# A two-layer encoder trunk: opening by halves of the features, another order of bands, halved weight splits and more banks

## The reference

```
cond = silu(c)
mod = cond @ ada_w[l] + ada_b[l]            # 6 groups of 1024: sh1 sc1 g1 sh2 sc2 g2
h = rms_norm(x, g) * (1 + sc1) + sh1
y = layer 0: stick-breaking heads (8) and sliding-window heads (8), one projection in, one out
    layer 1: HGRN2 gated linear recurrence (8 heads of 128), projections in and out
x = x + g1 * y
h = rms_norm(x, g) * (1 + sc2) + sh2
x = x + g2 * ((gelu(conv3(h @ W_gate)) * (h @ W_up)) @ W_down)      # width 2816
```

## Time and profile before

| | us |
|---|---|
| median of 3 runs | 1402.93 |
| their range | 1402.37 to 1403.20 |
| profiled execution | 1405.01 |
| its span | 1403.2 |
| TensorE busy | 1330.3 (95%) |
| VectorE busy | 810.3 (58%) |
| ScalarE busy | 554.9 (40%) |

### The profile page before, as it was taken

One profiled execution on the slowest core, in us unless ns is written; L12 is line 12 of the kernel. 1 busy time (PEld: TensorE's weight loads), 2 busy tenths in 40 slices (PEclk: granted clock), 3 DMA queues, 4 the chain that ended last, 5 costly groups with the idle time before them and its releaser, 6 DMA issues.

```text
span 1403.2 us, 17286 instructions
## 1 busy us (share of the span) xinstructions
PE 1330.3 (95%) x6208; PEld 1085.9 (77%) x6208; DVE 810.3 (58%) x1190; ACT 554.9 (40%) x831; POOL 49.7 (4%) x95
## 2 busy tenths in 40 slices
PE   4899996898999999999989999998999999999997
PEld 3677775676888888887868888887778888888785
DVE  6565356656666655535677777775665555452323
ACT  5455464324333333212155555553243333332213
POOL 1000000000000000000100000000000000000000
PEclk7799998999999999999989999999999999999999
DMA  9333431042545454464822222223523333333232
GB/s 362 109 114 87 127 119 50 1 137 88 161 138 146 141 154 142 136 192 138 269 62 76 75 75 65 72 61 96 174 75 90 99 95 94 100 91 104 79 101 75
DMA packets 189267, 160.37 MB, mean 114 GB/s; under 512 B 4959, under 2 KB 164920, under 8 KB 189218
## 3 DMA queue, kind: packets, MB, share of 16 engines
q1 hardware_dynamic: 177008, 116.41, 27.5%
q0 software_dynamic: 11936, 43.14, 9.9%
q10 hardware_dynamic: 274, 0.16, 0.0%
HBM read 157.59 MB, written 2.10 MB: 114 GB/s over the span
## 4 chain that ended last, share of the span: by engine, by line
PE 88%; DVE 4%; ACT 3%; DMA 1%; issue 1%; SPq 1%; DVEq 0%; ACTq 0%
PE proj L1372 59%; PE z L1372 22%; PE obank L1372 3%; PE misc L1372 2%; DMA w_raw<-ab_w_in 1%; SPq L439 1%; ACT w_hi L559 1%; DVE soft L1033 0%; DVE w_lo L881 0%; ACT q_sb L646 0%; ACT soft_a L646 0%; DVE hT_lo L1016 0%; DVE xT L1199 0%; DVE normed L1010 0%; PE z L1531 0%
## 5 line engine op out<-in xcount | busy, mean ns | idle before, releaser
L1372 PE MATMUL proj<-hT_hi,w_hi 128*128 128x512 f32 x1168 | 469.0, 402 | 18.3 <-DVE hT_lo L909 6.1
L881 DVE TENSOR_TENSOR w_lo<-w_raw,w_hi 128x1024 fp32r<-128x1024 f32 x198 | 242.4, 1224 | 384.6 <-ACT w_hi L559 384.6
L1372 PE MATMUL proj<-hT_lo,w_hi 128*128 128x512 f32 x1168 | 459.4, 393 | 0.0
L1372 PE MATMUL proj<-hT_hi,w_lo 128*128 128x512 f32 x1168 | 459.4, 393 | 0.0
L559 ACT ACTIVATE w_hi<-w_raw 128x1024 fp32r<-128x1024 f32 x198 | 209.6, 1059 | 505.0 <-PE proj L1372 318.6
L1372 PEld LDWEIGHTS proj<-hT_hi,w_hi 128*128 128x128 f32 x1168 | 221.9, 190 | 73.8 <-issue 22.5
L1372 PEld LDWEIGHTS proj<-hT_hi,w_lo 128*128 128x128 f32 x1168 | 222.3, 190 | 48.0
L1372 PEld LDWEIGHTS proj<-hT_lo,w_hi 128*128 128x128 f32 x1168 | 222.5, 191 | 45.3 <-issue 1.7
L1372 PE MATMUL z<-gated_hi,w_hi 128*128 (+1 forms) x352 | 140.9, 400 | 2.7 <-DVE xT L1199 2.7
L1372 PE MATMUL z<-gated_hi,w_lo 128*128 (+1 forms) x352 | 138.0, 392 | 0.0
L1372 PE MATMUL z<-gated_lo,w_hi 128*128 (+1 forms) x352 | 137.1, 389 | 0.0
(11 more groups left out here) (248 smaller groups left out, 1336.1 us busy)
## 6 DMA issues: line engine op xcount, KB each, us to landing
ada_raw<-ada_w POOLq DMA_DIRECT2D x80, 512.0 KB, 4.4
w_raw<-ffn_w_gate SPq DMA_DIRECT2D x44, 512.0 KB, 3.8
w_raw<-ffn_w_up SPq DMA_DIRECT2D x44, 512.0 KB, 4.0
w_raw<-ffn_w_down SPq DMA_DIRECT2D x44, 512.0 KB, 3.8
w_raw<-hg_w_in SPq DMA_DIRECT2D x32, 512.0 KB, 4.0
w_raw<-ab_w_in SPq DMA_DIRECT2D x18, 512.0 KB, 4.3
ada_first<-ada_w SPq DMA_DIRECT2D x7, 1024.0 KB, 17.3
w_raw<-ab_w_out SPq DMA_DIRECT2D x8, 512.0 KB, 4.4
```

Source lines behind the costliest of these rows:

```text
L881: nc.vector.tensor_tensor(w_lo[:, slot, :], w_raw[:, slot, :], w_hi[:, slot, :].bitcast(F32), ALU.subtract).then_inc(lo_done, 1)
L1372: return nc.tensor.matmul(dst, weights_ap, moving, start=start, stop=stop, skip_group_check=True)
```

## The change

- **Opening.** The rows of `ada_w` are assigned to partitions as (p k) in place of (k p), and c is loaded by a DMA of its own in the same order. The blocks of shift and scale are loaded as halves: block k of half h holds columns 512 h to 512 h + 511 of both groups (two pieces of 2 KB a partition). Order on SyncE: x, 8 blocks of half 0, the weights of four units (SQ, SK, SV, WK) for feature blocks 0 to 3, 8 blocks of half 1, the weights for feature blocks 4 to 7, the band table. `quad(0)` runs the four units over blocks 0 to 3 in banks proj[0], proj[1], obank, zb[0]; `quad(1)` the rest. Between them TensorE makes five of eight transposes of x, and one block (7) of half 1 goes through TensorE in place of VectorE. Scaled x goes to `x_hat`; ScalarE applies scale and shift in two passes, one for `normed` and one for `hT_hi`. Loads of later modulation groups wait for the end of quad(1).
- **Bands.** A new order of `STEPS0`. The window transposes of head 0 (S) come after the logits of heads 1 and 2; of the three modulation blocks behind A(7) one stands between the window's maxima and its normalisation, two behind it.
- **Halved splits.** Behind a pair, unit u+2 is split in two halves; the first waits only for the pair's block 3 (`pair_half`). In head 0 of the recurrence the split of u+3 moves ahead of the logarithm's scan, and `level_k` and `scores` are cleared by VectorE, before the split of u+4.
- **Banks.** Output units take four banks in turn; the second half of the down projection takes proj[0], proj[1], zb[0], zb[1].

```diff
-    ("u", SQ), ("u", SK), ("u", SV), ("A", 0), ("u", WK), ("T", 0), ("B", 0), ("u", WV), ("C", 0),
-    ("A", 1), ("u", SQ + 1), ("T", 4), ("B", 1), ("u", SK + 1), ("C", 1),
-    ("u", SV + 1), ("A", 2), ("u", WQ), ("T", 1), ("B", 2), ("u", WQ + 1), ("C", 2),
+    ("Q", 0), ("A", 0), ("T", 0), ("u", WV), ("B", 0), ("u", SQ + 1), ("T", 4), ("C", 0),
+    ("A", 1), ("u", SK + 1), ("B", 1), ("u", SV + 1), ("C", 1),
+    ("A", 2), ("T", 1), ("u", WQ), ("B", 2), ("u", WQ + 1), ("C", 2),
     ("A", 3), ("u", SQ + 2), ("B", 3), ("u", SK + 2), ("C", 3),
...
-    ("A", 6), ("u", WQ + 3), ("T", 3), ("B", 6), ("C", 6), ("A", 7), ("L", 0), ("B", 7), ("S", 0),
-    ("C", 7),
+    ("A", 6), ("u", SV + 3), ("B", 6), ("T", 3), ("u", WQ + 3), ("C", 6),
+    ("A", 7), ("L", 0), ("B", 7), ("C", 7),
...
+        out_banks = [proj[0], proj[1], zb[2], zb[3]]
+        down_banks = [[zb[0], zb[1], zb[2], zb[3]], [proj[0], proj[1], zb[0], zb[1]]]
...
+            def first_ada(h):
+                for k in range(DC):
+                    src = ada_w[0].rearrange("(p k) (g h n) -> p k g h n", k=DC, g=MODS, h=2)[:, k, 0:2, h, :]
+                    sp.dma_start(ada_first[:, DC * (1 - h) + k, :].rearrange("p (g n) -> p g n", g=2), src
+                                 ).then_inc(ada_first_in[h][k], 16)
...
+            first_ada(0)
+            quad_load(0)
+            first_ada(1)
+            quad_load(1)
+            sp.dma_start(table2, tables[:, 2 * P:9 * P]).then_inc(bands_in, 16)
...
+            def split_first(u):
+                act.wait_ge(raw_in[0], u * 8 + 48)
+                act.wait_ge(pair_half, BEHIND_PAIR[u])
+                nc.scalar.activation(w_hi[:, 0, 0:HALF_UNIT], w_raw[:, 0, 0:HALF_UNIT], ACT.Copy).then_inc(half_hi, 1)
...
+            for i in range(4):
+                first_block(0, i)
             dve.wait_ge(misc_full, MISC_AT["small1"] + 1)
             nc.vector.tensor_copy(small[:, 1, :], misc[:, 0:96]).then_inc(misc_free, 1)
...
+            for i in range(4, DC):
+                first_block(0, i)
+            dve.wait_ge(misc_free, MISC_AT["small3"] + 1)
+            split(0, 0)
+            first_columns(0)
+            split(1, 1)
+            for dc in range(HALVES0):
+                first_low(dc)
+                first_block(1, dc)
+            for i in range(HALVES0, len(VECTOR_BLOCKS[1])):
+                first_block(1, i)
+            split(2, 0)
+            first_columns(1)
+            split(3, 1)
+            for dc in range(HALVES0, DC):
+                first_low(dc)
...
+            dve.wait_ge(xt_full, DC)
             for hp in range(4):
                 nc.vector.memset(k_sb[HEAD:P, hp, :], 0.0).then_inc(k_clear, 1)
...
                 elif kind == "L":
                     window_max(0)
+                    ada_blocks(1)
                     window_norm(0)
-                elif kind == "S":
-                    window_copy(0)
+                    ada_blocks(HEAD_BLOCKS[SB_HEADS - 1] - 1)
...
+            first_norm(0)
+            x_rows(range(0, 3))
+            split(2, 0)
+            split(3, 1)
+            x_rows(range(3, DC))
+            first_norm(1)
...
+            x_columns(range(0, 3))
+            pe.wait_ge(first_used, DC)
+            misc_wait("first0")
+            first_sums(0)
+            quad(0)
+            x_columns(range(3, DC))
+            first_products()
+            pe.wait_ge(first_used, DC + len(VECTOR_BLOCKS[1]))
+            first_sums(1)
```

More of the change, by code:

```diff
@@ L167, in trunk @@
         hT_hi = sb("hT_hi", [P, DC, SEQ], F32R)
+        with ExitStack() as before:
+            x_hat = sb("x_hat", [P, DC, SEQ], F32, before)
         hT_lo = sb("hT_lo", [P, DC, SEQ], F32R)
@@ L757, in ffn @@
                                          h32[:, 0, :], ACT.Copy).then_inc(gp_hi, 1)
+                one(0)
+                with act.Fori(1, FB) as f:
+                    one(f)
             def down(u0, n, last=False):
@@ L1424, in unit_pair @@
                         last.then_inc(unit_mm, 1)
+                    elif s == 0 and k == DC // 2 - 1:
+                        last.then_inc(pair_half, 1)
             def norm_sum(n):
@@ L1478, in _, with first_sums @@
[L1478 to L1481 removed]
+            def first_sums(h):
+                for g in range(2):
+                    for dc in range(HALVES0):
+                        col, at = HALVES0 * g + dc, slice(g * 512 + dc * P, g * 512 + (dc + 1) * P)
+                        last = mm(misc[:, col:col + 1], ada_sum[:, h, at], ones[:, 0:1],
+                                  start=not (h and TENSOR_BLOCKS), stop=True)
+                last.then_inc(misc_full, 1)
@@ new lines, in quad @@
+            def quad(h):
+                his = (w_hi[:, 0, :], w_hi[:, 1, :]) if h == 0 else quad_hi
+                los = (w_lo[:, 0, :], w_lo[:, 1, :]) if h == 0 else quad_lo
+                for k in range(HALVES0):
+                    dc = HALVES0 * h + k
+                    pe.wait_ge(h_lo, dc + 1)
+                    for i in range(4):
+                        if k == 0 and i % 2 == 0:
+                            parts_ready(2 * h + i // 2)
+                        at = slice(512 * (i % 2) + k * P, 512 * (i % 2) + (k + 1) * P)
+                        hi, lo, dst = his[i // 2][:, at], los[i // 2][:, at], quad_banks[i][:]
+                        mm(dst, hi, hT_hi[:, dc, :], start=(dc == 0))
+                        mm(dst, hi, hT_lo[:, dc, :])
+                        last = mm(dst, lo, hT_hi[:, dc, :], stop=(dc == DC - 1))
+                        if dc == DC - 1:
+                            last.then_inc(unit_mm, 1)
+                if h == 0:
+                    last.then_inc(quad_half, 1)
@@ L1641, in ffn, with one @@
                     unit(u0 + 2 * f + 1, 1, proj[1][:])
+                one(1)
+                with pe.Fori(2, FB) as f:
+                    one(f)
             def down(layer, u0, n):
-                def one(u, slot, block, first=False, mod_group=None):
+                def one(u, slot, block, first=False, mod_group=None, banks=down_banks[0]):
                     parts_ready(u)
```

488 lines of the change are left out of this document (301 added, 187 removed).

## The result

The changed kernel takes 1389.57 us (median of 4 runs, 1387.75 to 1392.3) against 1402.65 for the one before on the same chip: ratio 0.9912, 95% interval 0.9889 to 0.9934. The direction was forecast rightly. The gain is 13.1 us where the sum had 25.2, and 1389.57 lies just above the range given (1367 to 1389). The profiled execution took 1388.26, its span 1384.8.

The account below looks back on a forecast made before the run. TensorE, busy 95% of the span, bounds the kernel through its stops and half clock. Gains 6.0 + 0.7 + 5.7 + 7.9 + 1.4 + 1.2 + 2.3 = 25.2 us take the median 1402.9 to 1377.7; range 1367 to 1389.

Parts of the forecast that it names:

- the step of the opening: Start of kernel: loading modulation by halves lets four units start early; gain 6.0 us, bounds 2 and 11.
- Rival E: Heads' end and later: half of Part 3 and Parts 4 returns as the next wait, 9.3 less gain, 1387.0 us; chance 0.12.
- Rival D: Opening: strided half-row loads run slow; at 130 GB/s the kernel takes about 1412 us; chance 0.03.
- quad(0) at 31.3, quad(1) at 50.3, A(0) done at 66.3: Opening: forecast times in us of both quads' starts and the first head's scores' end, behind the 6.0 us gain.
- Rival B: Opening gives nothing: both quads start cold, and extra waits eat the head start; 1383.7 us; chance 0.17.
- rival C: Opening gives 11 us as quads stay warm and small1 comes early, plus head 0 gains; 1370.7 us; chance 0.15.
- Part 2: Order of bands: the wait before C(6) goes, gain 0.7 us; no wait counted before a B.
- Part 3: End of the heads: earlier maxima and later window transposes let C(7) start 5.1 us earlier; gain 5.7 us in all.
- Parts 4: Halved splits behind pairs and more banks; both output projections lose waits of 4.9 us and cold clocks, gain 7.9 us.
- Head 0: Recurrence head 0: unit starts at 735.6 instead of 736.80 us, still waiting for q_hg; gain 1.2 us.
- the pairs' w_lo: Behind the three pairs: TensorE's waits for w_lo go, gain 1.4 us.
- Down halves: Second halves of the down projection: four waits for xT, 2.7 us, nearly go; gain 2.3 us.

Follow-up runs that it names:

- its faults mended: Changed kernel plus small1 copied early, all blocks on VectorE, unread matmuls in opening and late gaps, WK evacuated before units 4 and 5's low parts: 1376.84 us.
- c_now placed: c_now allocated among buffers living until the heads' end: changed kernel so edited 1385.13 us; the one with its faults mended 1373.84 us, ratio 0.9792.
- experiment 3: Changed kernel with small1 copied early and all blocks on VectorE, plus unread matmuls: behind the opening sums 1382.2 us; at late gaps only 1382.69 us.

## Why the prediction was wrong

What failed is the step of the opening, which I had at 6.0 us and the changed kernel at 0.6, and one cost that had no step at all, 2.8 us in the MLPs. Of the 12.1 us between sum and measured gain 6.8 are missing in the span, 1.6 lie outside it and 3.7 in which runs were profiled. None of the signs that I had named for being wrong came, but of the times forecast only quad(0) was near: quad(1), B(0) and C(7) came 4.6, 5.5 and 5.4 us late (54.91, 77.56 and 219.32). Rival E's 1387.0 lies nearest to the measured time, by luck: parts 3 and 4, of which it takes half back, gave 15.2 us of 18.5 in their stages. Point by point:

- **What bounds the kernel.** Held. Every microsecond found was a stop of TensorE, its half clock behind one, or, what I had excluded ("nothing in the change alters their number or rate"), the rate of its matmuls.
- **Transfers of half rows.** Held: 400 to 409 GB/s against the 400 taken. Rival D and the 164 GB/s estimated from the Trainium skill's batching rule ("DMA: Bandwidth & Descriptors", section Bandwidth) are refuted for queued loads.
- **quad(0) at 31.3, quad(1) at 50.3, A(0) done at 66.3.** This is the step that failed: 32.36, 54.91 and 71.64. The 5.3 us are quad(0)'s start 1.1, its longer cold run 1.05 (13.45 against 12.4), the stretch between the quads 2.5 (9.1 against 6.6), quad(1) 0.3 and A(0) 0.5. The start is late because two affine passes come 0.70 us apart and not 0.6, and the eight sums end at 29.5 and so the modulation at 29.9, not 29.2. Between the quads I had written "16 one-column matmuls (1.84)". A row x16 is a group of 8 in float32, two records each, and the change runs two such groups there: 1.84 for the products and 2.27 for the sums, 2.1 more than priced; the two passes of ScalarE behind them are most of the other 0.4. That row was in front of me with its count; the code's loop over 8 columns would have told it.
- **The two starts from cold.** Priced at 1.5 each; measured 1.7 to 3.1 (quads of 12.6 to 14.0 us against 10.9). Rival B was right in its reason (two cold starts with small work between). With its faults mended the opening gives 7.7 us net of c_now's cost, and with c_now placed 10.5 by the ratios (0.9867 against 0.9792, on two chips), so rival C's 11 us for a warm opening with small1 early was near.
- **Part 2.** No new wait before a B, and the wait before C(6) went. Held.
- **Part 3, 5.7.** C(7) moved by 5.1 as forecast and the first window transposes by 5.6, but the later window stages ran at half clock for a part (from 228.7 us) and gave 1.4 back.
- **Parts 4, output projections, 7.9.** Measured 4.3 and 3.8. Right in size, but I had it as one cause; it was two, the banks with 1.8 and 1.7 us and the early half with 1.2 and 1.1.
- **Head 0, 1.2, and the pairs' w_lo, 1.4.** The wait for q_hg is 2.19 us as forecast (about 2). The stage gives 2.3 in place of 1.7, of which 1.6 stand behind the pair (9.7 us to unit u+3 before, 8.0 after); and another 1.2 comes behind it, since unit u+3 takes 7.35 us in place of 8.51.
- **Down halves, 2.3.** The waits for xT are all gone, but the stages give 0.6 instead of 3.2 with the pairs' share. c_now's 64 bytes took 2.8. With c_now placed the two MLPs give 2.5 and 0.9, together 3.4. No row of the trace before could have shown it; that a new buffer ahead of the hot ones moves them was in the diff.
- **From one trace to the median.** The spans of before vary from 1398.4 to 1405.5 us in the 37 runs beside the experiments; the three longest have a mean granted clock of 0.972 or 0.973, as the profiled one has (0.973), most others 0.976 to 0.978. So a long run has more matmuls at half clock, and some of the gain read from one may have been such chance; no run separates it. The time outside the span grew by some 1.0 us at the median (2.1 to 3.5 in runs of the changed kernel). It is 1.8 to 2.0 with c_now placed or with no block on TensorE; why stays open.

## What to carry to other kernels

Count what a row's "x" means from the loop in the code before you price new work by it. A stop of TensorE costs its length and the cold start behind it, so price splitting a stretch in two by its starts, and where a gap can't be closed, fill it with matmuls that nobody reads. Put a new small buffer where it moves nothing hot, and compare the mean of the largest matmul groups after every change in allocation.

## What the runs showed of the hardware

- The spacing of TensorE's float32r matmuls depends on where the moving operand lies in SBUF: the same 264 matmuls show 390 ns or, after a shift by 64 bytes, 395, and a down projection of 528 takes 1.5 to 1.9 us more (128.59 to 130.10 and 121.68 to 123.54).
- The granted clock fell to half in the opening of the changed kernel at 51.2 us though TensorE had no idle time since 32.4 us; what it did from 45.81 us until it fell were 20 transposes and one-column matmuls. With no block on TensorE and two unread matmuls of 512 columns behind each group of sums (experiment 3) it stayed at 1.00.
- Transposes of float32 128x128 come 0.21 us apart at half clock and 0.11 at full clock, and in the kernel before the granted clock rose from 0.50 to 1.00 at 26.0 us while TensorE did nothing else (21.43 to 27.2 us).
- Queued loads in two pieces of 2 KB a partition, with eight rows from one partition to the next, moved at 400 to 409 GB/s, the pieces of 4 KB before mostly at 406 to 422.
